# Block products for the third unit of the second feed-forward's output matrix in the last quarter of both layers

## The reference, cut to what matters

```python
def sq_relu_mlp(xn, w_in, w_out):
    h = jax.nn.relu(xn @ w_in)
    return (h * h) @ w_out
...
        h = h + sq_relu_mlp(rms_norm(h, norm_mlp_g[i]), mlp_w_in[i], mlp_w_out[i])
    return rms_norm(h, norm_final_g)
```

## Time and profile before

| | |
|---|---|
| time, median of 3 runs | 1871.3 us (1871.23 to 1871.88) |
| span of the profiled execution | 1869.4 us |
| TensorE matmul busy | 1857.1 us (99%) |
| VectorE busy | 1329.9 us (71%) |
| ScalarE busy | 931.1 us (50%) |
| GpSimd busy | 101.9 us (5%) |
| HBM traffic | 94 GB/s over the span |

### The profile page before, as it was taken

How to read it: one execution, slowest core, us unless ns; L and a number is a source line. 1 busy time by engine, 2 the same in 40 slices (tenths; PEclk the granted TensorE clock), 3 DMA queues, 4 the chain that set the end, 5 groups by cost and what they waited for, 6 DMA issues and landing times.

```text
span 1869.4 us, 28026 instructions
## 1 busy us (share of the span) xinstructions
PE 1857.1 (99%) x10531; PEld 1541.6 (82%) x10531; DVE 1329.9 (71%) x1824; ACT 931.1 (50%) x1190; POOL 101.9 (5%) x90
## 2 busy tenths in 40 slices
PE   9999999999999999999999999999999999999998
PEld 7788878888888887877889898988778788989897
DVE  7767774677357667556577898947788658789884
ACT  6392464555133344444543554545667744445462
POOL 0010021000000021000100000020110010000001
PEclk9999999999999999999999999999999999999999
DMA  7223122322322234222232223334232133233321
GB/s 242 90 91 123 40 68 68 109 93 68 112 90 94 76 100 140 68 78 68 93 101 97 93 95 109 98 108 147 88 105 71 60 101 104 81 105 99 105 90 68
DMA packets 146801, 179.31 MB, mean 96 GB/s; under 512 B 3582, under 2 KB 140670, under 8 KB 144257
## 3 DMA queue, kind: packets, MB, share of 16 engines
q1 hardware_dynamic: 143296, 160.44, 26.2%
q0 software_dynamic: 3104, 17.10, 2.9%
q10 hardware_dynamic: 288, 0.26, 0.0%
HBM read 173.48 MB, written 2.20 MB: 94 GB/s over the span
## 4 chain that ended last, share of the span: by engine, by line
PE 94%; DVE 3%; ACT 1%; DMA 1%; issue 0%; SPq 0%; DVEq 0%; ACTq 0%
PE bank L1063 23%; PE bank L1065 23%; PE bank L1064 23%; PE bank L1500 5%; PE bank L1501 5%; PE bank L1502 5%; PE bank L1191 2%; PE bank L1805 2%; PE bank L1787 1%; PE bank L1197 1%; PE bank L1676 1%; PE bank L1677 1%; PE bank L1678 1%; PE bank L1611 1%; PE bank L1664 1%; DVE w_lo L1901 0%
## 5 line engine op out<-in xcount | busy, mean ns | idle before, releaser
L1063 PE MATMUL bank<-n_hi,w_hi 128*128 128x512 f32 x1054 | 425.0, 403 | 1.4 <-DVE w_lo L1901 1.3
L1065 PE MATMUL bank<-n_hi,w_lo 128*128 128x512 f32 x1054 | 417.7, 396 | 0.0
L1064 PE MATMUL bank<-n_lo,w_hi 128*128 128x512 f32 x1054 | 416.6, 395 | 0.0
L1895 ACT ACTIVATE w_hi<-raw 128x2048 fp32r<-128x2048 f32 (+2 forms) x117 | 218.8, 1870 | 371.9 <-PE bank L1065 369.3
L1901 DVE TENSOR_TENSOR w_lo<-raw,w_hi 128x2048 fp32r<-128x2048 f32 (+2 forms) x123 | 275.7, 2242 | 112.2 <-ACT w_hi L1895 110.2
L1064 PE MATMUL bank<-ff_lo,w_hi 128*128 128x512 f32 x784 | 309.0, 394 | 0.0
L1065 PE MATMUL bank<-ff_hi,w_lo 128*128 128x512 f32 x720 | 286.2, 397 | 0.0
L1063 PE MATMUL bank<-ff_hi,w_hi 128*128 128x512 f32 x720 | 284.4, 395 | 0.6 <-DVE ff_lo L2200 0.6
L1063 PEld LDWEIGHTS bank<-n_hi,w_hi 128*128 128x128 f32 x1054 | 198.0, 188 | 53.9 <-issue 5.0
L1064 PEld LDWEIGHTS bank<-n_lo,w_hi 128*128 128x128 f32 x1054 | 198.1, 188 | 48.8 <-issue 2.9
L1065 PEld LDWEIGHTS bank<-n_hi,w_lo 128*128 128x128 f32 x1054 | 197.9, 188 | 47.0
(11 more groups left out here) (455 smaller groups left out, 3015.2 us busy)
## 6 DMA issues: line engine op xcount, KB each, us to landing
raw<-in_mlp_w_in SPq DMA_DIRECT2D x32, 1024.0 KB, 5.4
raw<-in_mlp_w_out SPq DMA_DIRECT2D x32, 1024.0 KB, 5.1
raw<-in_w_up SPq DMA_DIRECT2D x22, 1024.0 KB, 5.1
raw<-in_w_units SPq DMA_DIRECT2D x14, 1024.0 KB, 4.8
raw<-in_a_w_qkv SPq DMA_DIRECT2D x12, 1024.0 KB, 5.1
raw<-in_b_w_qkv SPq DMA_DIRECT2D x12, 1024.0 KB, 5.2
b_bias<-bias_table POOLq DMA_DIRECT2D x16, 448.0 KB, 4.6
raw<-in_w_down SPq DMA_DIRECT2D x8, 768.0 KB, 4.6
```

Source lines behind the costliest of these rows:

```text
L1063: nc.tensor.matmul(b[:, :], w_hi[:, j % 2, cols], hi, start=start, stop=False)
L1064: nc.tensor.matmul(b[:, :], w_hi[:, j % 2, cols], lo, start=False, stop=False)
L1065: return nc.tensor.matmul(b[:, :], w_lo[:, j % 2, cols], hi, start=False, stop=final)
L1895: act.activation(w_hi[:, s, cols], raw[:, s, cols], ACT.Copy).then_inc(hi_ready, 1)
```

## The change

In quarters 3 and 7 too, the third unit of w_out is made of block products. `has_down` is now true for every quarter but the first of a layer, so `begun_down_tensor`, `block_tensor(pe, m, DOWN)` and `plain_down` replace `project(pe, p_dn[m], ...)` there, and `down_scalar` and `down_vector` run for them. In the last quarter these stop before the steps that belong to a following quarter: VectorE's eight additions move into the normalisation (`third_unit_added`) in place of `residual_group` for the second group's first unit, and ScalarE waits for the product S1 of the third unit before it writes squares (and n_hi) over what that product may still read. The semaphore counts, before worked out by formula, are now looked up in tables; that changes no instruction.

```diff
         def has_down(m):
-            return m % 4 in (1, 2)
+            return m % 4 > 0
...
+        def third_unit_added(dve, m):
+            first_added(dve, m, DOWN)
+            third_added(dve, m, DOWN)
+            second_added(dve, m, DOWN)
+            last_added(dve, m, DOWN)
...
             def input_part(part):
                 residual_part(act, n, part)
+                if n == 5 and part == 0:
+                    piece_used(act, 3, ("S1", DOWN))
...
             for part in range(2):
                 residual_part(act, 7, part)
+                if part == 0:
+                    piece_used(act, 7, ("S1", DOWN))
                 squared(act, 7, part)
...
             own_splits(dve, ph, split_lo)
             weighted(0, 4)
-            residual_group(dve, ph, ph.iters - 1, 0)
+            third_unit_added(dve, 7)
             weighted(4, 6)
...
                 own_splits(dve, ph, split_lo, (lambda: weighted_squares(dve, 0, 4)) if n == 2 else None)
-                residual_group(dve, ph, ph.iters - 1, 0)
+                if n == 5:
+                    third_unit_added(dve, 3)
+                else:
+                    residual_group(dve, ph, ph.iters - 1, 0)
                 low(*PARTS[1])
...
-            rounds(act, p_dn[first + 3], a_own, 0, split_hi, no_group)
...
             split_hi(act, ph.u0 + 3, 1)
-            for op in PIECE_OF_OP:
-                piece_high(act, m + 1, op, 0)
+            if m % 4 < 3:
+                for op in PIECE_OF_OP:
+                    piece_high(act, m + 1, op, 0)
...
-            residual(dve, p_dn[first + 3])
...
             split_lo(dve, ph.u0 + 3, 1)
+            if m % 4 == 3:
+                return
             first_added(dve, m, DOWN)
```

More of the change, by code:

```diff
@@ L771, in build @@
         PIECE_OF_OP = {"A1": ("A11", "A12"), "A22": ("A22",), "S23": ("S2", "S3"), "S14": ("S1", "S4")}
-        SPLITS = [(op, u) for u in range(UNITS) for op in ("A1", "S23", "S14")]
-        SPLITS += [(op, DOWN) for op in ("T4", "T2", "A1", "S23", "T3", "S14", "T1")]
-        SPLIT_AT = {op: n for n, op in enumerate(SPLITS)}
         T_SUMS = ("T1", "T3", "T2", "T4")
-        SUM_AT = [3 * u for u in range(BLOCKS)]
-        OPERANDS, SUMS = 4, KD + 4
+        OPERANDS = 4
+        DOWN_SPLITS = ("T4", "T2", "A1", "S23", "T3", "S14", "T1")
         def has_down(m):
-            return m % 4 in (1, 2)
-        def counted(m, each, short, begin):
-            layer, quarter = divmod(m, 4)
-            return layer * (begin + 2 * each + short) + (begin + (quarter - 1) * each if quarter else 0)
+            return m % 4 > 0
         def unit_index(m, u):
@@ L791, in unit_group, with count @@
             return p_in[m].g0 + u if u < UNITS else p_dn[m].g0 + 2
[L793 to L810, removed]
+        piece_count, split_count, sum_count, kept_count = {}, {}, {}, {}
+        def count(table, *key):
+            table[key] = len(table) + 1
+        for layer in range(2):
+            for n in range(KD + 4):
+                count(sum_count, 4 * layer, "operand", n)
+            if layer:
+                count(split_count, 4, "output_begun")
+            for n in range(OPERANDS):
+                count(split_count, 4 * layer, "operand", n)
+            for m in range(4 * layer + 1, 4 * layer + 4):
+                for u in range(BLOCKS if has_down(m) else UNITS):
+                    count(kept_count, m, u)
+                    for name in FACTORS:
+                        count(piece_count, m, name, u)
+                    for op in DOWN_SPLITS if u == DOWN else ("A1", "S23", "S14"):
+                        count(split_count, m, op, u)
+                    for n in (1, 2, 3):
+                        count(sum_count, m, u, n)
+                if has_down(m):
+                    for name in T_SUMS:
+                        count(sum_count, m, name)
+        PIECE_HI_ENDS = split_count[4, "output_begun"]
         def piece_split(eng, m, op, u, what):
@@ L2050, in operand_low @@
                              (t_tiles[:, half, :], ff_hi[:, spare, :], ff_lo[:, spare, :]))
[L2051 removed]
+            done(dve, dve.tensor_tensor(lo, whole, hi.bitcast(F32), ALU.subtract), at("piece_lo"), split_count[m, "operand", n])
         def unit_loaded(eng, v):
```

43 lines of the change are left out of this document (19 added, 24 removed).

## The result

| | before | after |
|---|---|---|
| time, median of 5 runs | 1871.9 us (1871.23 to 1874.73) | 1880.2 us (1879.03 to 1881.17) |
| ratio of the times | | 1.0043 (1.0030 to 1.0056) |
| span of the profiled execution | 1869.4 us | 1879.4 us |
| mean granted clock of TensorE | 0.999 | 0.996 |

The change costs 8.4 us. The forecast was 4.7 us and its range ended at 1878.4, so the time lies outside it.

The account below looks back on a forecast made before the run. TensorE, busy in 99% of the span, was taken to bound the kernel; 2.5 us lost at the layer boundary plus 2.2 at the end made 4.7 us slower, 1876.0 us from the 1871.3 median, range 1871.3 to 1878.4.

Parts of the forecast that it names:

- What the change takes off TensorE: Third and fourth unit of each last quarter: 21.41 us instead of 22.40, offering 0.99 us each, 2.0 us for both.
- The boundary: Between the layers: VectorE's queue delays w_lo, next layer starts 2.2 us later, second unit 0.3 more; 2.5 us lost.
- The hold: GpSimd's addition of squares blocks VectorE's third addition (hT<-hT,kept_rows, both inputs in SBUF) at the boundary, adding 1.9 us.
- the 0.3 us for the second unit: Next layer's second unit at the boundary: its w_lo comes late, costing 0.3 us (between 0 and 0.5).
- The end: Kernel's end: VectorE's last sum ends at 24.8, second small matmuls start at 26.3 instead of 24.1, 2.2 us later.
- Rival 1: GpSimd's additions cost nothing at either place: 0.3 us lost at boundary, 0.1 gained at end, 1871.5 us; chance 0.14.
- Rival 2: Gain arrives: w_lo ready by 21.4 at the boundary, end covered too, 2.0 us gained, 1869.3 us; chance 0.09.
- the sum of 4.7 us: Boundary 2.5 us plus end 2.2 us, both lateness of TensorE's starts; the main forecast, chance 0.56.
- rival 3: TensorE's clock falls in both new idle stretches: 2 us at boundary (1878.0), less than 1 at end; chance 0.17.

Follow-up runs that it names:

- the run with the new order and GpSimd's additions cut: After with VectorE's eight additions first, next w_lo ahead of n_lo of tiles 4 and 5, GpSimd's additions cut to 8 columns: 1870.0 us, ratio 0.9988.
- the mended pair: Two versions of after with VectorE's changed order, squares added by VectorE and the second unit's w_hi and w_lo moved forward: 1870.5 and 1870.6 us.
- the run with the clock held: After with 13 extra matmuls of constants behind the fourth output unit of both last quarters: 1875.2 us, ratio 1.0017.
- mended: After with VectorE's changed order, its own squares additions, the second unit's w_hi and w_lo earlier, third sum and h_w behind tile 6's addition: 1870.5 us, ratio 0.9993.
- the second version: The mended kernel with four h_w instead of five ahead of the addition of tile 7, four instead of three behind it: 1870.6 us, ratio 0.9992.

## Why the prediction was wrong

- **What the change takes off TensorE**: right. Third and fourth unit ended 21.4 us after the third began; the run with the new order and GpSimd's additions cut started there, at 21.4 in both places.
- **The boundary**: right in mechanism and size. The eight additions ended at 19.8 (forecast 19.7), w_lo at 24.6 (24.4), the next layer started at 24.7 (24.6), the idle was 3.1 us (3.2). The hold was on the row I had named, 2.65 us. With the clock taken out (13 extra matmuls) the second unit was 2.4 us late, forecast 2.5. In that sum the 0.3 us for the second unit were 0.1 (11.76 behind the first against 11.66), and I had let TensorE ask for it 11.2 us behind the first instead of 11.66.
- **The end**: right too, for the lateness. The last sum ended at 24.8 (forecast 24.8). With the clock taken out the second small matmuls came at 26.4 (26.3), and the end 2.3 us late, forecast 2.2. The hold on the four h_w (4.22 us for 2.06) and on the one of tile 6 (2.15 for 0.49) was there; the rows that I had named for it show only instructions with two SBUF inputs, and these have one. The row that bears on it was in the trace of before: four h_w at 1839.53 took 4.08 us beside GpSimd's addition of 1839.14.
- **Rival 1**, that GpSimd's additions cost nothing, fell with the cut additions: 0.69 us instead of 2.65, and 8.8 us less in the time. **Rival 2**, that the gain arrives, fell as the kernel stood. It needed 3.0 us less on VectorE, and it took a reorder and VectorE's own additions to find them.
- **The step that failed is the clock**: the sum of 4.7 us has no term for it. I had named it as rival 3 and given it 0.17; it is what happened, at both places, and it measured 4.1 us by the rows and 5.0 by the medians. I held against it that no row showed dense work, a pause and dense work again. That a row is missing is no evidence. The one row that bore on the question, the fall behind the last matmul, pointed to a fall, and so did the sentence of the Trainium skill ("TensorE: Matmul & The Clock Gate", Part 1) that I cited. The rows of after agree with that sentence in both directions: 0.50 after the pause, 0.92 and then 1.00 again under matmuls.
- **Its price was too low at the end.** For the boundary I had 2 us, and the rows gave 1.6, 1.6, 2.3, 2.6 and 2.8 in five kernels. For the end I had "less than 1", with "few matmuls left". It was 2.5 us in after (39.3 against 36.8 from the third unit to the end). The 28 transposes alone are 3.25 us of TensorE at full clock, and behind them stands the store; I had not read their row. The store gave little back when TensorE came sooner (the mended pair), but the loss in after was too large for it to hide. With 2.5 + 2.2 for the lateness, 1.6 and 2.5 for the clock, the sum is 8.8 us; 8.4 were measured. That it comes so close is partly luck, as the clock's price is taken from one execution and was 1.6 to 2.8 us at the boundary.

So the sum of 4.7 us was right for what it counted by the rows of the run with the clock held (4.7; by its median, 3.1 us), and the forecast was wrong because it left the clock to a rival.

## What to carry to other kernels

Where a change makes TensorE wait some 3 us behind dense matmuls, count the wait and then the half clock behind it, and read what TensorE has to do there: 1.6 to 2.8 us here on dense matmuls, 1.1 to 2.5 us where small ones and a store follow. Before giving VectorE more work near a GpSimd addition, add the whole time of each such addition that falls beside an instruction with two SBUF inputs to VectorE's queue (h_w, with one, was held as well; the additions with an input in PSUM were not), and remember that work which becomes ready sooner also calls GpSimd sooner. A shorter idle can be worth more than its length: 1.15 instead of 3.1 us kept the clock, and so did 2.9 us of useless matmuls in the gaps, which moved neither start.

## What the runs showed of the hardware beyond that

- The clock fell behind idle stretches of 3.1 to 5.6 us and, at the end of two kernels (squares added by VectorE, mended), among small matmuls with waits of 0.36 and 0.74 us; it did not fall behind 1.15 us at the boundary, nor at the end of the run with 13 extra matmuls, with a wait of 0.53 us ahead of the small ones, nor in the second version with waits of 0.29 and 0.32 us. How long it stayed at half differed between runs with the same wait (3.10 and 3.14 us, and 1.6 and 2.8 us lost). What decides that stays open.
- A matmul of 128 float32 columns of constants shows as two: 13 of them are 26 records, 0.11 us apart.
- GpSimd's addition of 16 elements took 0.22 us alone and 2.06 us beside VectorE's w_lo. It waited for the end of an instruction ten times its length. Addition of 128x1024 in SBUF takes 1.22 us on VectorE and 2.40 on GpSimd, so at the boundary the hold of one such addition (2.65 us instead of 0.69) cost VectorE more than the work itself would have.
